# A hybrid trunk layer with expert-choice MoE on one core: counting ranks for the expert two ahead inside the first products

## The reference

```python
def ec_moe(h, router_w, w1, w3, w2):
    xt = h.reshape(B * T, D)
    cap = EC_FACTOR * (B * T) // N_EXPERTS           # 128 rows for the latents, 16 for the context
    aff = jax.nn.softmax((xt @ router_w).astype(jnp.float32), axis=-1)
    gate_vals, idx = lax.top_k(aff.T, cap)           # each of 16 experts picks its rows
    xe = xt[idx]
    hid = jax.nn.silu(jnp.einsum('ecd,edf->ecf', xe, w1)) * jnp.einsum('ecd,edf->ecf', xe, w3)
    ye = jnp.einsum('ecf,efd->ecd', hid, w2) * gate_vals[..., None]
    y = jnp.zeros_like(xt).at[idx.reshape(-1)].add(ye.reshape(-1, D).astype(xt.dtype))
```

## Time and profile before

| | us |
|---|---|
| median of 3 runs (1629.03 to 1632.03) | 1630.45 |
| the profiled execution's own time | 1631.1 |
| its span | 1629.3 |
| TensorE busy | 1580.3 (97%) |
| VectorE busy | 716.6 (44%) |
| GpSimd busy | 477.5 (29%) |
| ScalarE busy | 387.4 (24%) |
| DMA, mean busy share in the expert stage | 0.89 to 0.96 |

### The profile page before, as it was taken

One profiled execution on the slowest core, in us unless ns is written; L12 is line 12 of the kernel. 1 busy time (PEld: TensorE's weight loads), 2 busy tenths in 40 slices (PEclk: granted clock), 3 DMA queues, 4 the chain that ended last, 5 costly groups with the idle time before them and its releaser, 6 DMA issues. The chain is left out here.

```text
span 1629.3 us, 28403 instructions
## 1 busy us (share of the span) xinstructions
PE 1580.3 (97%) x11180; PEld 1377.1 (85%) x11180; DVE 716.6 (44%) x1871; ACT 387.4 (24%) x970; POOL 477.5 (29%) x560
## 2 busy tenths in 40 slices
PE   6999999999999899999988999999999999999997
PEld 5866876666668767788878999999999999999997
DVE  4001046776565844222364244444334454433344
ACT  5210113341221466411131111111111111111114
POOL 3000000015232643121203343433344343334432
PEclk9999999999999999999999999999999999999999
DMA  9302212132202486423269899999899999999985
GB/s 346 114 11 85 82 39 59 36 125 30 59 29 93 133 239 204 157 66 103 91 212 353 290 299 297 316 322 298 278 293 304 291 315 329 299 286 285 315 263 228
DMA packets 225582, 324.85 MB, mean 199 GB/s; under 512 B 36015, under 2 KB 116008, under 8 KB 225466
## 3 DMA queue, kind: packets, MB, share of 16 engines
q1 hardware_dynamic: 185817, 282.70, 51.7%
q0 software_dynamic: 15568, 17.45, 5.7%
q10 hardware_dynamic: 24080, 23.02, 4.8%
HBM read 294.42 MB, written 25.51 MB: 196 GB/s over the span
## 5 line engine op out<-in xcount | busy, mean ns | idle before, releaser
L1973 PE MATMUL psum<-arena 128*128 128x144 f32 x4096 | 504.5, 286 | 1.7 <-DVE arena L2615 1.7
L1973 PEld LDWEIGHTS psum<-arena 128*128 128x128 f32 x4096 | 502.8, 190 | 1.9 <-ACT arena L1350 1.9
L1985 PE MATMUL psum<-arena 128*128 128x144 f32 x2048 | 257.3, 288 | 6.3 <-ACT arena L1391 5.0
L1985 PEld LDWEIGHTS psum<-arena 128*128 128x128 f32 x2048 | 254.8, 192 | 7.1 <-ACT arena L1391 5.2
L1556 PE MATMUL psum<-arena 128*128 128x384 f32 x720 | 242.9, 493 | 0.0
L889 POOL DMA_INDIRECT expert_list<-gt x128 | 129.8, 1014 | 317.2 <-DVE gt L2645 287.6
L1556 PEld LDWEIGHTS psum<-arena 128*128 128x128 f32 x720 | 134.5, 191 | 90.0 <-issue 2.9
L2675 DVE TENSOR_TENSOR arena<-gt,psum 128x144 f32<-128x144 f32 x128 | 38.8, 303 | 360.8 <-PE psum L1973 359.8
L2497 DVE SCALAR_TENSOR_TENSOR arena<-arena,gt 128x1024 f32<-128x1024 f32 x128 | 159.1, 1280 | 0.5 <-DMA arena<-affinity_rows 0.5
L1559 PE MATMUL psum<-arena 128*128 128x256 f32 (+2 forms) x784 | 146.4, 346 | 0.0
L1559 PEld LDWEIGHTS psum<-arena 128*128 128x128 f32 x784 | 129.4, 190 | 15.5 <-issue 1.7
(11 more groups left out here) (379 smaller groups left out, 1629.4 us busy)
## 6 DMA issues: line engine op xcount, KB each, us to landing
arena<-in_exp_w SPq DMA_DIRECT2D x96, 2048.0 KB, 11.8
arena<-in_ada_w SPq DMA_DIRECT2D x24, 1024.0 KB, 7.0
arena<-in_w_in SPq DMA_DIRECT2D x11, 1024.0 KB, 5.2
arena<-in_x_sample SPq DMA_DIRECT2D x16, 512.0 KB, 4.8
arena<-affinity_rows SPq DMA_DIRECT2D x16, 512.0 KB
arena<-m_decay_rows ACTq DMA_DIRECT2D x36, 128.0 KB, 3.2
arena<-decay_rows ACTq DMA_DIRECT2D x24, 192.0 KB, 3.4
out<-arena SPq DMA_DIRECT2D x9, 512.0 KB, 2.6
```

What stands on the lines that cost most here:

```text
L1973: ins = mm(bank[:, 0:SLOTS], w[:, k, col], xeT[:, k, :], start=(k == 0), stop=(k == KD - 1))
L1985: ins = mm(bk[4 + db % 2][:, 0:SLOTS], wslot[4 + db // 4][:, k, (db % 4) * P:(db % 4) * P + P], hid[:, k, :], start=(k == 0), stop=(k == K ...
```

## The change

- VectorE: in experts 1 to 13 `rank_begin(e + 2)` and the eight counts move from the second products into blocks 1 to 4 of the first products, two counts ahead of the multiply of each block. Expert 0 keeps the counts for expert 2 in its second products. No sixteenth list is counted.
- GpSimd reads the lists back itself (`load_list`, `load_quarters`), not SyncE, and scatters and reads list e+2 and gathers the rows of e+2 inside expert e, ahead of the adds of e.
- Expert 1: GpSimd reads its list once as whole rows, gathers whole rows into `xg`, and TensorE turns them between expert 0's first and second products. Its list in quarters (needed for the adds) is read behind the gather.
- SyncE sends `load_row(e + 2)` ahead of slab 4 of expert e, behind a wait for the ranks of e + 1.

```diff
         def listed(e):
-            return 64 * e + 1 if not isinstance(e, int) or e < NE - 1 else 64 * (NE - 2) + 17
+            return 64 * e + 16 if not isinstance(e, int) or e < NE - 1 else 64 * (NE - 2) + 32
         def fetched(e):
-            return 64 * e + 16 if not isinstance(e, int) or e < NE - 1 else 64 * (NE - 2) + 32
+            return 64 * e - 32 if not isinstance(e, int) or e < NE - 1 else 64 * (NE - 3) + 48
...
-            load_list(1)
             load_row(2)
             for e in range(1, NE):
                 for q in range(6):
...
+                    if q == 4 and e + 2 < NE:
+                        load_row(e + 2)
                     expert_slab(e, q)
-                if e + 1 < NE:
-                    load_list(e + 1)
-                    load_row(e + 2)
...
             scatter_list(1)
+            def load_list(e, rows=False):
+                pool.wait_ge(list_sc, 16 * NL * e)
+                pool.sem_inc(idx_set, 1)
+                if rows:
+                    o = 2 if e == 1 else 8 * e
+                    pool.dma_start(lists[:, o:o + 2], list_d[0:P, :]).then_inc(list_in, 16)
+                else:
+                    load_quarters(e)
+            def load_quarters(e):
+                for c in range(4):
+                    dst = lists[32 * c:32 * c + 32, bass.ds(e * 8, 8)].rearrange("p (a w) -> p a w", w=2)
+                    pool.dma_start(dst, list_d[0:P, :].rearrange("(a i) w -> i a w", i=32)).then_inc(list_in, 16)
+            load_list(1, rows=True)
...
-            expert_rows(0, y_rows=True)
-            with pool.Fori(1, NE - 2) as e:
-                expert_rows(e)
-            expert_rows(NE - 2, x_rows=True)
-            pool.wait_ge(list_sc, 16 * NL * NE)
+            fetch_rows(1)
+            load_quarters(1)
+            pool.wait_ge(list_in, listed(1))
+            scatter_list(2)
+            load_list(2)
+            fetch_quarters(2)
+            add_rows(0)
+            with pool.Fori(1, NE - 3) as e:
+                added_free(e - 1)
+                scatter_list(e + 2)
+                load_list(e + 2)
+                fetch_quarters(e + 2)
+                add_quarters(e, e * 12 + 15)
+            e = NE - 3
+            added_free(e - 1)
+            scatter_list(e + 2)
+            load_list(e + 2, rows=True)
+            fetch_rows(e + 2)
+            add_quarters(e, e * 12 + 11)
+            added_free(e)
+            add_quarters(e + 1, e * 12 + 15)
+            added_free(e + 1)
...
             for e in range(NE - 1):
                 hidden(e)
-                if e == NE - 2:
-                    pe.wait_ge(xgl_in, fetched(NE - 1))
+                if e in (0, NE - 2):
+                    pe.wait_ge(xgl_in, fetched(e + 1))
                     pe.wait_ge(e_yeA, e + 1)
                     pe.wait_ge(e_yeD, e + 1)
                     x_turn_latent(0, KD)
...
             def rank_begin(e):
-                dve.wait_ge(list_in, listed(e - 1))
+                if not isinstance(e, int) or e > 1:
+                    dve.wait_ge(list_in, listed(e - 1))
...
+                early = not (is_first or is_last or x_rows)
                 for fb in range(KD):
                     if is_first and fb < 3:
                         rank_count(1, ((0, 1, 2), (3, 4, 5), (6, 7))[fb])
+                    if early and fb == 1:
+                        rank_begin(e + 2)
+                    if early and 1 <= fb < 5:
+                        rank_count(e + 2, (2 * fb - 2, 2 * fb - 1))
                     dve.wait_ge(e_sil, e * KD + (fb + 1))
...
-                    if fb == KD - 2 and not (is_first or is_last or x_rows):
+                    if fb == KD - 2 and not (is_last or x_rows):
                         x_turned(e + 1)
-                if is_first:
-                    x_turned(e + 1)
...
-                    rank_begin(e + 2)
+                if is_first:
+                    rank_begin(2)
                 for db in range(1, KD, 2):
-                    if not is_last:
-                        rank_count(e + 2, (db - 1, db))
+                    if is_first:
+                        rank_count(2, (db - 1, db))
```

78 lines of the change are left out of this document (37 added, 41 removed).

## The result

The changed kernel takes 1653.53 us, the median of four runs (1647.04 to 1666.22), against 1631.12 us before (now of four runs too; the 1630.45 of the prediction was that of three). The ratio is 1.0149 (95% interval 1.0087 to 1.021): 22 us slower where +3.4 us was forecast, and beyond the end of the range, 1642.5. The four runs of after lie 19 us apart, those of before 3 us. The profiled execution of after is the quickest, 1647.04 us with a span of 1645.3 us: 16.0 us over the span of before, 1629.3.

The account below looks back on a forecast made before the run. TensorE was taken to bound the expert stage. Losses after of 12.9 us (0.9 + 1.7 + 0.2 + 7.4 + 2.7) against 9.5 before gave +3.4 on 1631.1, less 0.65: 1633.9 us, range 1624.5 to 1642.5.

Parts of the forecast that it names:

- (a): Expert 1's rows turned by TensorE after expert 0's first products: idle 1.7 us, transposes 0.9 us, old 7.8 us loss gone.
- Too short to touch the clock: The 1.7 us idle ahead of expert 1's transposes was claimed not to lower TensorE's granted clock.
- (b): Counting for expert 2 in expert 0's second products, waiting for four quarter-list reads: 0.2 us lost (0 to 2).
- (c): Counts inside first products: expert 1's block 3 waits for list 2, idle 7.4 us plus 2.7 us of clock.
- S: The start of expert 1's first products, from which the forecast counted when list 2 would be there.
- For e = 2 ... not late. In the steady state ... 13 us of lead: Lists in the loop arrive before VectorE asks: S + 52 against S + 62 in expert 2, later 13 us of lead.
- rival 3: GpSimd's loop becomes the bound: round 42.5 us of 47.04; at 50 us 26 us slower, 1660; chance 0.03.
- none in later experts: TensorE's timeline was to show no stop in experts after expert 1's first products.
- (e): Gathers fetched an expert ahead: VectorE's waits for them go and 1.7 us are won.
- What is late next is nothing on TensorE: With gathers an expert ahead, nothing further was to be late on TensorE.
- the later stalls: Later experts' 1.21 us idle and one slow set of second products in before, 1.7 us together, forecast to go.
- rival 1: Expert 1's stall for list 2 isn't there, the wait met in time: -6.7 us, 1623.8; chance 0.12.

Follow-up runs that it names:

- e9: Changed kernel with scatters split by the adds' wait, expert 1's counts later, and expert 1's first weight slabs held until its rows landed: ratio 0.9964 to before.
- e10: e6 with the list reads given back to SyncE: ratio 0.0023 from that of e6, intervals overlapping.
- e6: Changed kernel with four of an expert's eight list scatters issued before GpSimd's wait for the last adds, four behind it: 15 us faster than the changed kernel.
- e8: Changed kernel with both edits, scatters split by the wait for the adds and expert 1's counts in blocks 3 to 6: 1629.5 us, ratio 0.9977 to before.
- e3: Kernel before with only expert 1's rows gathered whole and turned by TensorE, its list read once more by SyncE: 1628.6 us.
- e2: Kernel before, the first four list scatters also waiting for the second half of the ranks, so eight go in one run: 64.2 us idle before second products; median not given.
- e7: Changed kernel, the last four list scatters issued only when the first four have landed: GpSimd's round 51.96 us; slow, median not given.
- e5: The changed kernel unedited, run again for a second profile: profiled execution 1650.8 us, ratio interval 1.0083 to 1.0159.
- e4: Changed kernel with expert 1's counts for expert 3 in blocks 3 to 6 of the first products, not 1 to 4: 1663 us by the median.
- e11: Changed kernel with all eight list scatters ahead of GpSimd's wait for the last adds: almost as fast as e6; median not given.
- e13: Changed kernel with weight slabs of experts 2 to 15 cut to 32 KB instead of 2.1 MB: 1637 us.
- e15: Kernel before with expert 1 turned by TensorE alone and expert 1's first slabs held until its rows landed: 1626.3 us, ratio 0.9965.
- e1: Kernel before with GpSimd waiting behind each expert's eight list scatters until all have landed: 137 us slower than before.

## Why the prediction was wrong, step by step

**(a), 1.7 + 0.9 us: short by 3.2 us** (1.95 us won where 7.8 - 2.6 = 5.2 were forecast). GpSimd in after:

```profile
871.93 0.61 POOL L892 DMA_DIRECT2D gt<-expert_list  x1 [5.28 <-DMA expert_list<-gt]
877.12 0.18 POOL L918 CAST gt<-gt 128x1 int32<-128x1 f32 x1 [4.59 <-DMA gt<-expert_list]
877.58 1.00 POOL L920 DMA_INDIRECT arena<-h_latent,gt  x1 [0.27 <-POOL gt L918]
```

The issue was too dear in the sum (0.61, not 1.28), the landing too cheap (4.59, not 2.7; in e9, with expert 1's slabs held back, it took 1.85), and the scatters landed 0.9 us later; the gather's 6.8 us were right. Idle 3.05. "Too short to touch the clock" failed as well: 2.40 us of idle left it at 1.00 in before, 3.05 here was followed by 0.91 over the next 17.12 us, some 1.4 us. The transposes took 0.3 us more.

**(b), 0.2 us:** no stop there. Right.

**(c), 7.4 + 2.7 us: right in place, releaser and size.** 6.49 us of idle ahead of block 3, released by VectorE's multiply, which stood behind the copy of the gates:

```profile
919.06 0.17 DVE L2667 COPY gt<-gt 128x8 f32 x1 [10.07 <-DMA gt<-expert_list]
```

List 2 was there at S + 15.4 (919.06 - 903.66), forecast S + 16.0, but from two misses that cancel: issue 4 x 0.57 instead of 4 x 1.28 us, landing of scatters and list longer (5.64 and 3.48 against 4.4 and 2.7). A transfer that the nearest row prices by its engine was in truth cheap to issue and dear to land. Its clock cost 2.2, forecast 2.7. For the Trainium skill's rule against the move ("DMA: Bandwidth & Descriptors", "Issuing engine by pattern") no run shows a price at this stop: e10 undid the move and kept the stop, 6.57 us.

**"For e = 2 ... not late. In the steady state ... 13 us of lead" and rival 3: the round was right, its use was not.** GpSimd's round in after is 42.6 us where it isn't held up (first scatters at 939.62 and 982.22); the sum was 42.5, with the same two misses in its terms, which cancel again. I used it only to ask whether a list comes late. It comes in time. What it decides besides is where in the expert the scatters stand.

**The step that failed** is the one that put the moved scatters beside TensorE's work at no cost: "none in later experts", and in (e) "What is late next is nothing on TensorE". It costed moved DMAs by their issue and their landing alone. Before scatters an expert's list in two fours with a gap of 1.3 or 2.7 us; the change has the ranks ready early, so eight go out in one run, beside 2.1 MB slabs, and TensorE's semaphore reaches ScalarE and VectorE late, 2.6 us in most experts and 5.5 us in expert 1's second products. That is all but free in first products and costs 1.8 to 6.7 us in second products, clock included. In the profile it made the 6.7 us of expert 1; the 3.8 us of single stops in three first products stand beside such runs too and have no releaser. These 10.5 us are most of the 12.6 by which the profile (+16.0) missed the forecast (+3.4); (a)'s 3.2 and 1.0 at the end come on top; (c) gives 1.4 back, and (b) and the later stalls (2.1 us, forecast 1.7) 0.6. It explains the size of the loss and not its direction: with most of it taken out (e6) the changed kernel is still slower, 1.0036 or some 6 us, near the forecast. With (c) out as well (e8) it is at 0.9977, 3.8 us faster than before, where rival 1 gave 6.7 for a kernel without (c)'s stop.

Shown, on chips 1 and 10: that the lateness grows with the length of the run (in the kernel before 1.8 us with fours, e3, and 2.6 to 5.2 with eights, e2; in the changed kernel at most 1.4 with a landing between the fours, e7, and 2.6 or more in most experts with eights, e5), and that it stops TensorE in second products (e4). Shown too: that a shorter round of GpSimd with its scatters in the first products takes 12 to 15 us off (e6, e11). Not shown: why it happens, whether it needs the slabs' traffic, why chip 14 doesn't have it, and what the changed kernel as it is takes there. What the executions of after above 1650.8 us lost is open too.

## What to carry to other kernels

A step that is moved off the critical path still has a place: ask which stage it will stand beside, and whether that stage has the slack to take its side effects, here 3.92 us a block in the first products and 1.96 in the second. When a stop is taken out, ask what had used it to catch up; e4 lost a 6.5 us stop and gained nothing, since 30 us of other stops came in its place. Before a cause is called shown, look in the same profile for a stretch that the edit left as it was: expert 0 in e13 told that the chip had changed with the edit. And cost the parts of a change apart: the one that helped here (expert 1 turned by TensorE) is worth some 4 us alone (e3) and 5.5 us by the median (e15) with one wait that keeps weights out of the way of a small transfer on the critical path.

## What the runs showed of the hardware

- Eight indirect scatters of 128 x 8 bytes in one run on GpSimd, beside transfers at 93% of the DMA engines: what TensorE announces behind about the fifth scatter reaches ScalarE and VectorE only 1.1 to 1.8 us behind the last one, 2.6 us late in expert 5 of after and 5.5 us late in expert 1's second products. With a gap of 1.4 us in the middle the lateness is 1.4 us (e6, e11); with fours 2.7 us apart it is up to 1.8 us (e1, e3), with the landing waited for between the fours up to 1.4 (e7). On chip 14 and in the profile of before it is nil everywhere.
- A plain transfer issued by GpSimd costs it 0.57 to 0.61 us, less than an indirect one (0.97 + 0.30).
- Landing of eight such scatters: 3.7 to 6.3 us beside the weights (after), 1.9 us with the DMA engines at 19% (e13, expert 5; in its expert 0, beside whole slabs, 5.25). The Trainium skill ("DMA: Bandwidth & Descriptors", "Anatomy of one DMA — SWDGE (gpsimd) path") says that the semaphore update follows the confirmed write and can be surprisingly long behind when the target is HBM. The landings agree with it as far as they go.
- A read of 128 rows of 8 bytes took 5.2 us from issue to use with fresh slabs in the queue, 2.5 us with those held back.
